# Entry of a streaming encoder step: norm weight spread by TensorE, zero blocks one per unit, small loads behind ring tiles

## What is computed

```
h = rms_norm(x, norm_mix)                 # x * rsqrt(mean(x*x) + 1e-6) * norm_mix
z = h @ w_in                              # 1024 x 8208, cut into the columns below
qa, ka, va, ra, da, qb, kb, vb, ga, gb = jnp.split(z, offsets, axis=-1)
log_a = log_sigmoid(da @ w_decay + b_decay) / 16
o_a   = gla_scan(qa, ka, va, log_a, s0)   # gated linear attention, 4 heads
u_a   = (rms_norm(o_a, gla_norm) * silu(ra)) @ w_proj_a
u_b   = (rms_norm(diff_attention(qb, kb, vb), diff_norm) * 0.8) @ w_proj_b
x     = x + (sigmoid(ga) * u_a + sigmoid(gb) * u_b) @ w_out
x     = x + hmoe(rms_norm(x, norm_ffn))   # top-1 of 4 groups, then top-2 of 4 experts
y     = rms_norm(x, norm_final)
```

## Time and profile before

| | before |
|---|---|
| median of 3 runs | 1068.31 us (1067.98 to 1071.55) |
| the profiled execution's own time | 1070.26 us |
| its span (first to last instruction) | 1068.4 us |
| mean granted TensorE clock | 0.979 |
| TensorE busy | 1013.4 us (95%) |
| weight loads beside it | 903.3 us (85%) |
| DVE busy | 664.4 us (62%) |
| ACT busy | 539.6 us (51%) |
| POOL busy | 165.0 us (15%) |
| chain that ended last | TensorE 80%, DMA 8%, DVE 5%, ACT 3% |

### The profile page before, as it was taken

The page is one execution under the profiler, slowest core; times in us unless marked ns, Lnnn a source line. Parts: engine busy times, 40 slices in busy tenths (PEclk is TensorE's granted clock), DMA queues, the critical chain, the costliest instruction groups (busy, mean ns, idle before and its releaser), DMA issues.

```text
span 1068.4 us, 16967 instructions
## 1 busy us (share of the span) xinstructions
PE 1013.4 (95%) x6946; PEld 903.3 (85%) x6946; DVE 664.4 (62%) x1008; ACT 539.6 (51%) x719; POOL 165.0 (15%) x178
## 2 busy tenths in 40 slices
PE   2899999999999999999999999999899999999984
PEld 2899989999899988888888899877788888888863
DVE  4232772344322356776766656356898989898976
ACT  5133742423222244455475543233678787878853
POOL 4000000400000032333241020013201010101061
PEclk8799999999999999999999999999999999999988
DMA  9662464884454567564454271616999999999856
GB/s 315 104 90 41 79 80 80 193 300 61 77 86 76 119 134 75 76 44 80 99 178 143 90 239 49 236 80 245 415 412 414 413 415 413 415 413 415 325 113 161
DMA packets 126313, 208.07 MB, mean 195 GB/s; under 512 B 11244, under 2 KB 68588, under 8 KB 126240
## 3 DMA queue, kind: packets, MB, share of 16 engines
q1 hardware_dynamic: 110432, 149.90, 51.4%
q0 software_dynamic: 13168, 47.59, 13.0%
q10 hardware_dynamic: 2640, 9.57, 2.2%
HBM read 174.92 MB, written 32.12 MB: 194 GB/s over the span
## 4 chain that ended last, share of the span: by engine, by line
PE 80%; DMA 8%; DVE 5%; ACT 3%; issue 3%; POOL 1%; DVEq 0%; ACTq 0%; SPq 0%; POOLq 0%
PE ps L1210 22%; PE ps L1212 22%; PE ps L1211 22%; PE ps L1190 5%; DMA ring<-in_w_in_dram 2%; DMA x<-y_rows,rows_i 2%; PE ps L1368 2%; PE ps L1382 2%; DMA x_rows<-h,slot_i 1%; ACT w_hi L827 1%; PE ps L1344 1%; PE ps L1328 1%; PE ps L1483 1%; POOL x L757 1%; PE ps L1343 1%
## 5 line engine op out<-in xcount | busy, mean ns | idle before, releaser
L1913 DVE TENSOR_TENSOR e_lo<-raw,e_hi 128x2048 fp32r<-128x2048 f32 x96 | 219.3, 2287 | 28.6 <-ACT e_hi L1007 28.4
L1007 ACT ACTIVATE e_hi<-raw 128x2048 fp32r<-128x2048 f32 x96 | 184.0, 1918 | 55.0 <-PE ps L1212 44.0
L1210 PE MATMUL ps<-h_hi,w_hi 128*128 128x272 f32 x640 | 191.2, 299 | 11.2 <-DVE w_lo L1687 7.6
L1212 PE MATMUL ps<-h_hi,w_lo 128*128 128x272 f32 x640 | 186.5, 291 | 0.0
L1211 PE MATMUL ps<-h_lo,w_hi 128*128 128x272 f32 x640 | 186.1, 291 | 0.0
L1210 PEld LDWEIGHTS ps<-h_hi,w_hi 128*128 128x128 f32 x640 | 122.6, 192 | 12.9 <-issue 8.8
L827 ACT ACTIVATE w_hi<-ring 128x1024 fp32r<-128x1024 f32 (+1 forms) x56 | 79.6, 1422 | 99.4 <-PE ps L1212 70.8
L1700 DVE TENSOR_TENSOR w_lo<-ring,w_hi 128x2048 fp32r<-128x2048 f32 (+1 forms) x40 | 72.5, 1811 | 86.8 <-ACT w_hi L827 86.8
L1211 PEld LDWEIGHTS ps<-h_lo,w_hi 128*128 128x128 f32 x640 | 122.7, 192 | 0.2
L1212 PEld LDWEIGHTS ps<-h_hi,w_lo 128*128 128x128 f32 x640 | 122.3, 191 | 0.0
L1210 PE MATMUL ps<-w_hi,h_hi 128*128 128x256 f32 x384 | 110.1, 287 | 2.5 <-DVE va L1984 2.5
(11 more groups left out here) (423 smaller groups left out, 2038.0 us busy)
## 6 DMA issues: line engine op xcount, KB each, us to landing
raw<-in_w_gate_dram SPq DMA_DIRECT2D x32, 1024.0 KB, 11.0
raw<-in_w_up_dram SPq DMA_DIRECT2D x32, 1024.0 KB, 9.7
raw<-in_w_down_dram SPq DMA_DIRECT2D x32, 1024.0 KB, 9.9
ring<-in_w_in_dram SPq DMA_DIRECT2D x24, 1024.0 KB, 11.1
x_rows<-zero POOLq DMA_DIRECT2D x16, 512.0 KB, 13.3
ring<-in_w_in_dram SPq DMA_DIRECT2D x16, 512.0 KB, 8.4
xg<-x_rows POOLq DMA_DIRECT2D x15, 512.0 KB, 6.2
y_rows<-yo ACTq DMA_DIRECT2D x14, 512.0 KB, 6.5
```

Source lines behind the costliest of these rows:

```text
L1007: act.activation(e_hi[buf][:], raw[slot][:], ACT.Copy).then_inc(s_ehi, 1)
L1210: pe.matmul(out, left[0], right[0], start=first, stop=False)
L1212: return pe.matmul(out, left[1], right[0], start=False, stop=final)
L1913: dve.tensor_tensor(e_lo[slot][:], raw[slot][:], e_hi[buf][:].bitcast(F32), ALU.subtract).then_inc(s_elo, 1)
```

## The change

- `norm_mix` is loaded as one row of 4 KB (`g_one`). TensorE multiplies a row of ones by it, two f32 matmuls of 512 columns into banks 0 and 1, and DVE copies the 1024 columns to `g_row` ahead of its first tile.
- SP asks for the first ring tile after x tile 0 instead of 1. Seven small loads go behind ring tile 3 (ahead of tile 4), the ten others ahead of the first ra tile (tile 8). "small" moves from the first ka unit to the fifth (unit 12); a new hook "more", behind the first ra unit (28), has DVE's two steps on diff_norm and the router weights.
- The state load waits for unit 3's end (a count of 4), and each of the 24 zero blocks for one more unit, from a count of 5. They all come ahead of the wait for `s_ke_mm`.
- Tile 2 is turned into banks 2 and 3, and the sample tile into 6 and 7, so tile 2 doesn't wait, and tile 3 waits for the first h_lo.
- Unit 0 starts when `w_hi` is there and does its 16 matmuls by `w_hi` first, then waits for `w_lo`. The sample tile is turned inside unit 1, after six of its eight chunks; ACT makes h_hi 4 ahead of w_hi 1, and DVE h_lo 4 ahead of w_lo 1.

```diff
-        hook(units_of["ka"][0], "small")
+        hook(units_of["ka"][4], "small")
+        hook(units_of["ra"][0], "more")
@@ SP
-            sp.dma_start(g_row[:], norm_mix.broadcast_to([P, D])).then_inc(s_gmix, 16)
-            sp.wait_ge(s_x[1], 16)
+            sp.dma_start(g_one[:], norm_mix).then_inc(s_gmix, 16)
+            sp.wait_ge(s_x[0], 16)
...
-                if n == RING:
+                if n == 2 * RING:
                     small_loads()
+                if n == stage_tile["ra"]:
+                    more_small_loads()
@@ POOL
             def zero_blocks(some):
-                for rows, at_row in some:
+                for k, (rows, at_row) in enumerate(some):
+                    pool.wait_ge(s_unit, 5 + k)
                     pool.dma_start(...).then_inc(s_zero, 16)
             step(pool.memset(zero[:], 0.0))
-            zero_blocks([(x_rows, ROWS * e) for e in range(NE // 2)])
             pool.dma_start(x_rows[NE * ROWS:NE * ROWS + 1]..., zero[0:2]).then_inc(s_zero, 16)
+            pool.wait_ge(s_unit, 4)
+            pool.dma_start(S_in[:], state_gla[0, 0].rearrange("h k v -> k h v")).then_inc(s_sin, 16)
+            zero_blocks([(x_rows, ROWS * e) for e in range(NE)] + [(y_rows, LATE + CAP * i) for i in range(NOVF)])
+            pool.dma_start(y_rows[LATE + CAP * NOVF:]..., zero[0:2]).then_inc(s_zero, 16)
             pool.wait_ge(s_ke_mm, NTILE)
-            zero_blocks([(x_rows, ROWS * e) for e in range(NE // 2, NE)] + [(y_rows, LATE + CAP * i) for i in range(NOVF)])
-            pool.dma_start(y_rows[LATE + CAP * NOVF:]..., zero[0:2]).then_inc(s_zero, 16)
-            pool.dma_start(S_in[:], state_gla[0, 0].rearrange("h k v -> k h v")).then_inc(s_sin, 16)
@@ ACT
-                b = 4 + 2 * (i % 2)
+                b = (4, 6, 2, 4, 6)[i]
...
             x_high(3)
+            x_high(4)
             take_apart(1)
-            x_high(4)
@@ TensorE
-                if i >= 2:
-                    pe.wait_ge(s_hT, i - 1)
+                if i >= 3:
+                    pe.wait_ge(s_hT, i - 2)
...
             pe.wait_ge(s_const, 1)
+            pe.wait_ge(s_gmix, 16)
+            for b in range(2):
+                last = pe.matmul(ps[:, b], ones[0:1], g_one[:, 512 * b:512 * b + 512], start=True, stop=True)
+            last.then_inc(s_gmix, 1)
...
-                if u == 1:
-                    x_turn(NTILE - 1)
                 if u == 2:
                     pe.wait_ge(s_hT, NTILE)
-                if d["first"]:
+                if u == 0:
+                    pe.wait_ge(s_hi, 1)
+                elif d["first"]:
                     pe.wait_ge(s_lo, n + 1)
...
+                    if u == 0:
+                        for c in range(KC):
+                            pe.matmul(ps[:, bank, 0:HALF], w[0][:, c, feats], x[0][:, c, cols], start=c == 0, stop=False)
+                            pe.matmul(ps[:, bank, 0:HALF], w[0][:, c, feats], x[1][:, c, cols], start=False, stop=False)
+                        pe.wait_ge(s_lo, 1)
+                        for c in range(KC):
+                            last = pe.matmul(ps[:, bank, 0:HALF], w[1][:, c, feats], x[0][:, c, cols], start=False, stop=c == KC - 1)
+                    for c in range(KC if u else 0):
+                        if u == 1 and c == 6:
+                            x_turn(NTILE - 1)
@@ DVE
             step(dve.memset(att[:], 0.0))
+            dve.wait_ge(s_gmix, 17)
+            step(dve.tensor_copy(g_row[:], ps[:, 0:2].rearrange("p b n -> p (b n)")))
...
-            x_low(4)
+                    x_low(4)
```

More of the change, by code:

```diff
@@ L169, in build @@
         g_row = at("g_row", 193952, [P, D])
+        g_one = at("g_one", 198048, [1, D])
         h_s = lamt[:].rearrange("p a b -> p (a b)").rearrange("p (c t) -> p c t", t=TS)
@@ L304, in build @@
         s_gmix, s_small = sem("s_gmix"), sem("s_small")
-        s_wcode = sem("s_wcode")
+        s_more = sem("s_more")
         s_const = sem("s_const")
@@ L521, in _, with more_small_loads @@
             dram = {"w_in": w_in, "w_proj_a": w_proj_a, "w_proj_b": w_proj_b, "w_out": w_out}
+            def more_small_loads():
+                with nc.allow_non_contiguous_dma("a few parameter columns"):
+                    for h in range(GH):
+                        sp.dma_start(g_gla[:, 2 * h:2 * h + 2], gla_norm[0].rearrange("(c p) -> p c", p=P)).then_inc(s_more, 16)
+                    sp.dma_start(g_diff, diff_norm[0].rearrange("(c p) -> p c", p=P)).then_inc(s_more, 16)
+                    sp.dma_start(g_ffn, norm_ffn[0].rearrange("(c p) -> p c", p=P)).then_inc(s_more, 16)
+                    sp.dma_start(wr[:, :, 0:NG], w_router_group[0].rearrange("(c p) n -> p c n", p=P)).then_inc(s_more, 16)
+                    sp.dma_start(wr[:, :, NG:NG + NE], w_router_expert[0].rearrange("(c p) n -> p c n", p=P)).then_inc(s_more, 16)
+                    sp.dma_start(br[:, 0:NG], b_router_group.broadcast_to([P, NG])).then_inc(s_more, 16)
+                    sp.dma_start(br[:, NG:NG + NE], b_router_expert.broadcast_to([P, NE])).then_inc(s_more, 16)
@@ L523, in small_loads @@
             def small_loads():
                 with nc.allow_non_contiguous_dma("a few parameter columns"):
-                    for h in range(GH):
-                        sp.dma_start(g_gla[:, 2 * h:2 * h + 2], gla_norm[0].rearrange("(c p) -> p c", p=P)).then_inc(s_small, 16)
-                    sp.dma_start(g_diff, diff_norm[0].rearrange("(c p) -> p c", p=P)).then_inc(s_small, 16)
                     sp.dma_start(b_dec, b_decay[0].rearrange("(c p) -> p c", p=P)).then_inc(s_small, 16)
-                    sp.dma_start(g_ffn, norm_ffn[0].rearrange("(c p) -> p c", p=P)).then_inc(s_small, 16)
@@ L535, in small_loads @@
[L535 to L540 removed]
+                    sp.dma_start(w_code[:], w_in[0, :, C_CODE:C_CODE + RANK].rearrange("(c p) n -> p c n", p=P)).then_inc(s_small, 16)
@@ L541, in load_wo @@
+                    sp.dma_start(w_dec[:], w_decay[0]).then_inc(s_small, 16)
+            sp.dma_start(g_one[:], norm_mix).then_inc(s_gmix, 16)
+            sp.wait_ge(s_x[0], 16)
             def load_wo(k):
@@ L860, in _ @@
             x_high(3)
+            x_high(4)
             take_apart(1)
-            x_high(4)
             def do(what, i=0):
                 if what == "small":
-                    act.wait_ge(s_wcode, 96)
+                    act.wait_ge(s_small, 16 * 7)
                     act.activation(wc_hi[:, :, 0:RANK], w_code[:], ACT.Copy).then_inc(s_lame, 1)
@@ L1492, in _ @@
                     feats, cols = slice(P * a, P * a + P), slice(HALF * b, HALF * b + HALF)
-                    for c in range(KC):
+                    if u == 0:
[8 more added lines that the diff above has]
+                            x_turn(NTILE - 1)
                         if kind == "pa" and d["nth"] == 0 and c % 4 == 0:
@@ L1737, in do @@
                         dve.tensor_scalar(t2[:, f, TP:NT], bT[:, f, TP:NT], bT[:, f, NT - 1:NT], -1.0, ALU.subtract, ALU.mult).then_inc(s_delta, 1)
+                elif what == "more":
+                    dve.wait_ge(s_more, 16 * 10)
+                    step(dve.tensor_scalar(g_diff_s, g_diff, 1.0 - LAM_INIT, None, ALU.mult))
+                    step(dve.tensor_tensor(wr[:], wr[:], rep(g_ffn, 2, NG + NE), ALU.mult))
                 elif what == "dec_apply":
```

14 lines of the change are left out of this document (3 added, 11 removed).

## The result

The changed kernel takes 1055.21 us, the median of four runs (1055.09, 1055.33, 1059.67, 1054.17), against 1068.14 for the kernel before on the same chip (four runs): a ratio of 0.9879, 95% interval 0.9852 to 0.9905. A second set of six runs on another chip has a median of 1057.56 and a ratio of 0.9885 (0.9864 to 0.9906). The median of all ten is 1056.8. The forecast was 1056.5.

A forecast was written before the change was run, and what follows sets the result against it. TensorE was taken as the bound, its start held by late ring tiles. Unit 0 6.3, sample tile 3.2 and clock 2.3 summed to 11.8 us: 1070.26 becomes 1058.5 profiled, median 1056.5, range 1052.5 to 1061.

The forecast's parts named there:

- forecast case: Whole kernel: 11.8 us won before unit 4, clock low at unit 0; own range 1054.5 to 1058.5, chance 0.58.
- first low stretch: TensorE in units 0 and 1 at the lower clock: kept by the main forecast; its removal priced at 1.9 us.
- The norm row: Entry: matmuls 4.0 us and DVE copy 1.2 replace the 512 KB broadcast; DVE's first reciprocal 2.1 us later, about 10.25.
- Unit 0: TensorE's first unit: starts at about 20.1 instead of 26.36, bound by DVE and ACT, 6.3 us won.
- the rival had it up: Units 0 and 1 at the full clock through the early matmuls, saving 1.9 us plus 0.7 on turns: 1054; chance 0.12.
- The sample tile, 3.2 us: Before unit 2: turning it in unit 1, its halves first, cuts the wait from 3.5 us to about 0.3.
- second low stretch: TensorE from 39.0 to 44.2 us at clock 0.50, dropped by the pause before unit 2: removing it wins 2.3 us.
- The two reasons for the late tiles: Entry: SP's queue with 17 small DMAs, and contention from zero blocks holding 41.7% of DMA engine time from 4 to 20 us.
- The first tile: First ring tile: lands between about 14 and 17.4 us instead of 21.98, before ACT is free for it.
- The rival that this tile is late: First ring tile lands behind x at 20 to 21, unit 0 starts at 23: 1059.5; chance 0.12.
- Small loads and zero blocks after: Later ring tiles: seven loads some 7 us, ten 6 to 10, landings below 16 us; cost to TensorE nil.
- the slower rival: A zero block per unit holds every ring tile, decided at a landing of 19.9 us: 1095; chance 0.06.

The follow-up runs named there:

- e11: The changed kernel profiled again with no edit, six runs on another chip: median 1057.56 us, ratio 0.9885; code product copied at 77.12 us (75.81 in the first profile).
- e6: The changed kernel with the norm row's matmuls waiting only for the ones and the 4 KB, not the masks: 1052.28 us, ratio 0.9843.
- e5: The changed kernel with unit 0 waiting for both halves of its tile again: code product copied at 79.98 us, 1063.00 us profiled, a single run.
- e1: The changed kernel with the norm row broadcast by DMA to 128 partitions again, no matmuls or DVE copy for it: 1055.74 us, ratio 0.9869.
- e4: The changed kernel with the sample tile turned ahead of unit 1 and its halves behind the second tile's, as before: 1058.22 us, ratio 0.9910.
- e2: The changed kernel with eight of the 24 zero blocks back at the entry and the state load behind the blocks: 1058.11 us, ratio 0.9893.
- e10: The changed kernel with eight zero blocks back at the entry and all small loads ahead of the third ring tile: 1066.70 us profiled, a single run.
- e7: The kernel before with only the zero blocks moved to one per unit and the state load to unit 4: 1060.35 us, ratio 0.9927.
- e8: The kernel before with only the small loads moved, all 17 behind the fourth ring tile: 1071.19 us, ratio 1.0017.
- e3: The changed kernel with all 17 small loads issued behind the second ring tile, ahead of the third, again: 1057.55 us, ratio 0.9894.

## Why the prediction was right, and where it was wrong

**Direction and size: right.** 11.8 us forecast, 13 measured in medians, 15.2 in the profiled pair; both medians, 1055.21 and 1057.56, and that of all ten lie in the forecast case's own range. The 3.4 that the profiled pair has more are the first low stretch (1.9), 0.9 behind the milestone, and 0.4 on unit 0 and the pause, with 0.2 left over. With the clock low at unit 0, as the forecast case had it, the milestone is 12.9 earlier (e11). So the total came out close partly by luck: the clock term was unsettled, and the wait that the new order was to remove had gone for another reason. (By its own terms the lower end of the stated range is 1052.2, not 1052.5; nothing hangs on it.)

**The norm row: right, term by term.** 4.0 forecast for the matmuls, 3.78 measured; 1.2 for the copy, 1.22; the first reciprocal at 10.25, 10.18. TensorE was indeed at the lower level there, while the granted-clock column says 1.00. The Trainium skill (TensorE: Matmul & The Clock Gate, Part 1: The HAM clock gate) has the throttled state as the default; the trace agrees with it in the duration, and by the column the price would have been 2.2. What the prediction didn't see is that the wait in front of the matmuls was not needed: it took the 5.0 us of trimask as given, and e6 shows 2 us lying there.

**Unit 0: right.** 20.1 forecast, 19.95 measured, and bound by DVE's h_lo, as stated. That the two halves need not both be there is worth 2.3 to 2.9 (e5).

**The clock at unit 0: half right.** The forecast case had it low, the rival had it up with 0.12. Both happen with the same kernel; it was up in the profile of the result, and in six of the ten profiles with it. The rival's chance should have been about a half, its price (1.9 plus 0.7) was too high: 1.3 at the milestone between two profiles of one kernel. The turns' 0.7 lie beside DVE's chain, as unit 0 starts at 19.95 and 19.96 either way, and the low stretch in e11 was 14 matmuls and not 18. Its reason, the norm matmuls, is not needed, by e1. And the argument against it, that TensorE has mostly nothing to do between turns and unit 0, held in four profiles only: its 1.2 us before unit 0 was the same at either level (only e4 with 1.3 and e5 with 3.5 had another), and the one before the last turns differed (1.1 to 1.8 us with the clock up, 0.6 to 0.8 with it low, as the turns ahead took longer). In the kernel before, the clock had fallen by 16.9, behind a pause of 1.7 us and ahead of the 7.3 us of idle time; so a pause of 1.7 us stood before a fall there, and pauses of up to 1.8 us stood before none here. What decides it stays open.

**The sample tile, 3.2 us: right sum, wrong cause.** The pause is gone, and with it the second low stretch (2.3), as forecast. But the step credited it to the new order of turn and halves. e4 takes the order back and has no pause; what took it away is the second ring tile, landed at 22.8 instead of 34.40. The order is an insurance for a late tile: in e2 and e10, with the tile at 30.5 to 30.7, unit 2 does not wait, but unit 3 does (2.5 and 0.9 us), behind the eviction of unit 0.

**The two reasons for the late tiles: one of them was wrong.** The prediction named SP's queue and contention side by side without a price for each. e7 and e8 give it: zero blocks 11.0 us, small loads nothing. The prediction priced the move of the small loads only by what it could cost, and e8 shows that it gains nothing by itself, because the third tile is not what TensorE waited for. e10 against e2 shows that it does have a worth where the blocks are at the entry and the rest of the change is in: the two share one cover.

**The first tile: right.** Forecast in by 14 to 17.4, measured 13.9. Of what held it to 21.98 before, the blocks are the larger part: in e7 the broadcast is there, the request is at 7.51 as before, and the tile is in by 16.0; in e8, with the blocks too, at 21.5. The rival that this tile is late did not come; even e2 has it by 16.9. The Trainium skill (DMA: Bandwidth & Descriptors, Anatomy of one DMA) fits 2.0 us plus bytes over 436 GB/s for DMAs that GpSimd issues, an estimate of 4.4 us for a tile. These tiles are issued by SP, beside other traffic, and the figure doesn't carry over: the quickest ring landing in the first 30 us of the changed kernel was 9.0.

**Small loads and zero blocks after: nil, right, with smaller reserve.** The seven loads took 13.6 us to issue (31.27 to 44.83) where 7 were forecast, and the ten 14.2 (92.11 to 106.27) for 6 to 10: the DMA engines were not quiet, zero blocks ran beside the loads. Ring landings were forecast below 16 and went to 19.7, and to 22.0 in e11. The step that failed here is the point at which the slower rival was to decide, 19.9: it counts to the moment at which ACT begins w_hi, not to the unit that needs it. Three tiles show that there is cover behind it. Tiles in e11 (22.0) and e6 (22.7) landed past that point, and e3's third w_hi began 4.7 late, all without a wait of TensorE. At 25.4 (e1) TensorE did wait, 1.4 us.

## What to carry to other kernels

Put a price on each suspected cause of a late load by moving one at a time: of two that were both visible in the trace, only the bulk writes beside the loads held the tile that TensorE waited for. Bulk writes that nobody needs soon can be released one by one by the compute's own progress, and their bound is the landing time of the loads beside them, not their own. Where two delays share one cover, removing either can look worthless or free by itself: put both back together before you say what one is worth. When a small operation is put at the start of a chain, look at what its first wait really needs: here a wait for masks that it doesn't use cost 2 of its 5 us.

## What the runs showed of the hardware

The granted clock at the first unit differs between executions of one kernel with the same timeline up to 0.1 us: 1.00 in one profile, 0.50 in another, worth 1.3 us (75.81 and 77.12). Which it is can be told from the turns ahead of it, 4.2 to 4.8 us for 24 of them or over 5.1, and not from the clock column, which reads 1.00 over both. Later stretches scatter as well: from 120 to 130 us the column has 0.83 in the changed kernel, 0.66 in e1 and 1.00 in e11. The scatter of the totals goes with it: over the ten runs of the changed kernel the time falls as the mean granted clock rises, from 1059.7 and 1059.8 us at 0.982 over 1056.8 at 0.987 to 1052.3 at 0.993. What sets the clock in one run no run here isolates.

Writes beside a pair of 1 MB loads hit the second much harder here: the zero blocks added 2.8 us to the first tile's flight and 7.8 to the second's (9.5 and 17.9 us without them, 12.3 and 25.7 with them, e2).

The time that column loads of a few KB take to issue depends on what is around them: the four gla_norm loads took 19.44 us to issue beside the entry's traffic, 10.04 in e7, 5.84 in the changed kernel and 1.96 in e3.
